# A hybrid decoder trunk: score masks as one product and one reduction, gates and row scale on ScalarE

## What is computed

```
def hgrn2(q, f_raw, i, g, lb, norm_w):
    f = lb + (1.0 - lb) * jax.nn.sigmoid(f_raw.astype(jnp.float32))
    log_f = jnp.log(f)
    k = 1.0 - f
    ...                       # scores_ij = sum_d q_id k_jd exp(cum_i - cum_j), j <= i
def mamba2(...):
    ...
    y = y.reshape(b, l, M_DIM) * jax.nn.silu(z.astype(jnp.float32))
    y = rms_norm(y.reshape(b, l, M_GROUPS, M_DIM // M_GROUPS)).reshape(b, l, M_DIM)
    return y * norm_w
```

## Time and profile before

| | |
|---|---|
| median of 3 runs | 2497.19 us (2496.18 to 2498.99) |
| the profiled execution's own time | 2498.01 us |
| its span, from the first to the last instruction | 2496.2 us |
| busy TensorE | 2392.7 us (96%) |
| busy VectorE | 1934.9 us (78%) |
| busy ScalarE | 1158.8 us (46%) |
| busy GpSimd | 167.4 us (7%) |

### The profile page before, as it was taken

How to read it: one execution, slowest core, us unless ns; L and a number is a source line. 1 busy time by engine, 2 the same in 40 slices (tenths; PEclk the granted TensorE clock), 3 DMA queues, 4 the chain that set the end, 5 groups by cost and what they waited for, 6 DMA issues and landing times.

```text
span 2496.2 us, 32892 instructions
## 1 busy us (share of the span) xinstructions
PE 2392.7 (96%) x13077; PEld 2071.0 (83%) x13077; DVE 1934.9 (78%) x2130; ACT 1158.8 (46%) x1504; POOL 167.4 (7%) x120
## 2 busy tenths in 40 slices
PE   2599999999999999999999999999999999999998
PEld 2599988888888888888879998888888888888886
DVE  7889898877898898889886578778888565655657
ACT  0264475545434435434436446655543443443442
POOL 0002100010011011010010110001001101101001
PEclk9999999999999999999999999999999999999999
DMA  9998577877898898999866546678788666656663
GB/s 388 393 336 300 148 267 261 292 273 270 291 345 308 290 348 306 316 315 313 296 201 177 155 118 202 225 261 282 253 289 301 188 190 193 186 189 192 186 192 119
DMA packets 205054, 633.78 MB, mean 254 GB/s; under 512 B 20237, under 2 KB 20965, under 8 KB 203621
## 3 DMA queue, kind: packets, MB, share of 16 engines
q1 hardware_dynamic: 200320, 614.80, 73.1%
q0 software_dynamic: 3008, 16.32, 1.7%
q10 hardware_dynamic: 1572, 0.56, 0.1%
HBM read 629.50 MB, written 2.10 MB: 253 GB/s over the span
## 4 chain that ended last, share of the span: by engine, by line
PE 90%; DVE 5%; DMA 2%; issue 1%; ACT 1%; SPq 0%; DVEq 0%; ACTq 0%
PE PS L1658 46%; PE PS L1684 17%; PE PS L1686 8%; PE PS L1626 8%; PE PS L1667 4%; DMA RAW<-in_w_ada 2%; PE PS L1640 2%; DVE ACC L1082 1%; DVE WL L1091 1%; PE PS L1715 1%; PE PS L1558 1%; PE PS L1591 1%; DVE CV L1298 0%; DVE ACC L985 0%; DVE MS L1315 0%
## 5 line engine op out<-in xcount | busy, mean ns | idle before, releaser
L686 ACT ACTIVATE WH<-RAW 128x1024 fp32r<-128x1024 f32 (+1 forms) x800 | 831.8, 1044 | 1082.6 <-PE PS L1658 554.6
L1091 DVE TENSOR_TENSOR WL<-RAW,WH 128x1024 fp32r<-128x1024 f32 (+1 forms) x800 | 992.0, 1247 | 431.8 <-ACT WH L686 430.6
L1684 PE MATMUL PS<-HT,WH 128*128 128x512 f32 x1792 | 632.5, 398 | 0.0
L1686 PE MATMUL PS<-HT,WL 128*128 128x256 f32 x1792 | 502.5, 280 | 0.0
L1684 PEld LDWEIGHTS PS<-HT,WH 128*128 128x128 f32 x1792 | 336.5, 188 | 82.3 <-issue 0.5
L985 DVE SCALAR_TENSOR_TENSOR ACC<-ADR,CT,ACC 128x1024 f32<-128x1024 f32 x300 | 392.0, 1307 | 12.3 <-DMA ADR<-in_w_ada 10.4
L1658 PE MATMUL PS<-WH,T2h 128*128 128x512 f32 x1208 | 374.2, 391 | 0.0
L1658 PE MATMUL PS<-WL,T2h 128*128 128x512 f32 x1208 | 372.1, 389 | 0.0
L1658 PE MATMUL PS<-WH,T2l 128*128 128x512 f32 x1208 | 372.0, 389 | 0.0
L1686 PEld LDWEIGHTS PS<-HT,WL 128*128 128x128 f32 x1792 | 338.4, 189 | 0.7 <-issue 0.5
L1658 PE MATMUL PS<-WH,HT 128*128 128x512 f32 x1024 | 288.7, 395 | 0.6 <-issue 0.6
(11 more groups left out here) (297 smaller groups left out, 2035.1 us busy)
## 6 DMA issues: line engine op xcount, KB each, us to landing
RAW<-in_w SPq DMA_DIRECT2D x512, 512.0 KB, 4.1
ADR<-in_w_ada SPq DMA_DIRECT2D x320, 512.0 KB, 5.5
RAW<-in_w_in SPq DMA_DIRECT2D x192, 512.0 KB, 3.9
RAW<-in_w_ada SPq DMA_DIRECT2D x64, 512.0 KB, 15.9
RAW<-in_w_out SPq DMA_DIRECT2D x64, 512.0 KB, 4.9
RAW<-in_w_in SPq DMA_DIRECT2D x32, 264.0 KB, 2.7
GB<-in_b_ada POOLq DMA_DIRECT2D x8, 512.0 KB, 7.3
LNG<-in_ln_g POOLq DMA_DIRECT2D x4, 1024.0 KB, 6.9
```

The lines of the kernel that those rows point to most:

```text
L686: act.activation(WH[:, wh_slot(layer, n), 0:w], RAW[:, k, 0:w], ACT.Copy).then_inc(hi_done.sem, 1)
L1091: tt(WL[:, k, 0:w], RAW[:, k, 0:w], WH[:, wh_slot(layer, n), 0:w].bitcast(F32), ALU.subtract).then_inc(lo_done.sem, 1)
L1684: mm(bank(p, j)[:, :], WH[:, wh, cols], HT[:, kt, :, :], start=kt == 0, stop=False, skip_group_check=True)
L1686: ins = mm(bank(p, j)[:, SEQ:2 * SEQ], WL[:, wl, cols], HTh[:, kt, :], start=False, stop=kt == KT - 1, skip_group_check=True)
```

## The change

The mask becomes one product over both PSUM banks (MS is written whole), and one `tensor_reduce` that adds the eight levels, reading MS with the level as the innermost index: neighbouring elements of the sum lie 128 floats apart. The gates go to ScalarE at (1,2), the logarithm moves from (1,4) to (1,3), the complement goes to ScalarE at (1,10). The scaling of XS goes to ScalarE at (7,4). The semaphores and their counts stay.

```
-                        if at == (1, 4):
+                        if at == (1, 2):
+                            act.wait_ge(set_free.sem, set_free.at(layer, 1))
+                            for h in range(4):
+                                fh = EQ[:, 2 * h:2 * h + 2, :]
+                                act.activation(fh, fh, ACT.Identity, bias=cLB[:, h:h + 1], scale=cOML[:, h:h + 1]
+                                               ).then_inc(hg_f.sem, 1)
+                        if at == (1, 3):
                             act.wait_ge(hg_f.sem, hg_f.at(layer, 4))
                             act.activation(E[:, :, :], EQ[:, :, :], ACT.Ln).then_inc(hg_lnf.sem, 1)
+                        if at == (1, 10):
+                            act.activation(KTt[:, :, :], EQ[:, :, :], ACT.Identity, bias=1.0, scale=-1.0
+                                           ).then_inc(hg_k.sem, 1)
...
+                        if at == (7, 4):
+                            act.wait_ge(rs_out.sem, rs_out.at(layer, 3))
+                            for b in range(4):
+                                xs = XS[:, b // 2, (b % 2) * 512:(b % 2 + 1) * 512]
+                                ins = act.activation(xs, xs, ACT.Copy, scale=RR[:, b:b + 1])
+                            ins.then_inc(m_rows.sem, 1)
...
                 dve.wait_ge(hg_s.sem, hg_s.at(layer, i + 1))
-                for b in range(2):
-                    ins = tt(MS[:, 4 * b:4 * b + 4, :], work(p, 2 + b)[:, :].rearrange("p (l i) -> p l i", i=P),
-                             LM[:, b * 512:(b + 1) * 512].rearrange("p (l i) -> p l i", i=P), ALU.mult)
-                ins.then_inc(hg_ms.sem, 1)
+                at = 4 * (1 - p % 2) + 2
+                tt(MS[:, :, :], PS[:, at:at + 2, :].rearrange("p b (l i) -> p (b l) i", i=P),
+                   LM[:, :].rearrange("p (l i) -> p l i", i=P), ALU.mult).then_inc(hg_ms.sem, 1)
                 dve.wait_ge(hg_ms.sem, hg_ms.at(layer, i + 1))
                 if i:
                     dve.wait_ge(hg_o.sem, hg_o.at(layer, i))
-                link(tt(MS[:, 0:4, :], MS[:, 0:4, :], MS[:, 4:8, :], ALU.add))
-                link(tt(MS[:, 0:2, :], MS[:, 0:2, :], MS[:, 2:4, :], ALU.add))
-                tt(SM[:, :], MS[:, 0, :], MS[:, 1, :], ALU.add).then_inc(hg_sm.sem, 1)
+                dve.tensor_reduce(SM[:, :], MS[:, :, :].rearrange("p l i -> p i l"), AX.X, ALU.add
+                                  ).then_inc(hg_sm.sem, 1)
...
-                        if at == (1, 3):
-                            dve.wait_ge(set_free.sem, set_free.at(layer, 1))
-                            for h in range(4):
-                                fh = EQ[:, 2 * h:2 * h + 2, :]
-                                ts(fh, fh, cOML[:, h:h + 1], cLB[:, h:h + 1], ALU.mult, ALU.add
-                                   ).then_inc(hg_f.sem, 1)
-                            dve.wait_ge(hg_f.sem, hg_f.at(layer, 4))
-                            ts(KTt[:, :, :], EQ[:, :, :], -1.0, 1.0, ALU.mult, ALU.add).then_inc(hg_k.sem, 1)
...
-                            dve.wait_ge(rs_out.sem, rs_out.at(layer, 3))
-                            for b in range(4):
-                                xs = XS[:, b // 2, (b % 2) * 512:(b % 2 + 1) * 512]
-                                ins = ts(xs, xs, RR[:, b:b + 1], None, ALU.mult)
-                            ins.then_inc(m_rows.sem, 1)
```

## The result

| | before | after |
|---|---|---|
| median of 5 runs each, us | 2497.19 | 2507.74 |
| lowest and highest run, us | 2495.17 to 2498.99 | 2506.25 to 2510.64 |
| profiled execution, us (its span) | 2498.01 (2496.2) | 2510.64 (2508.8) |

The changed kernel is slower: its time is 1.0042 times that of before, with an interval of 1.0031 to 1.0052, or +10.5 us. The prediction was 2496.9 us with a range up to 2502.5. It was wrong.

A forecast was written before the change was run, and what follows sets the result against it. TensorE, busy 2392.7 of 2496.2 us, was taken as the bound, so only its idle time could change. Mask -4.85, gates +3.55 and row scale +1.0 gave -0.3 us on the median 2497.19: 2496.9 us, range 2494.5 to 2502.5.

The forecast's parts named there:

- Part 1: Score mask: one product and one reduction of 1.22 us each end TensorE's waits for SM; -4.85 us.
- the stops at pass 4: First unit of pass 4, each layer: TensorE's 0.29 us stop for the product of mask 7 goes.
- rival (A): Score mask: the strided reduction is slow, 2.29 us at half rate; total +4.4, 2501.6 us; chance 0.19.
- Rival (B): Score mask: the reduction stops for GpSimd as the addition did; mask gives -1.5 us, total 2500.3 us; chance 0.07.
- Rival (D): Score mask: it gets shorter, but TensorE waits as long for something else; total 2501.7 us; chance 0.05.
- Part 2: Forget gates, logarithm and complement: ScalarE's late split makes TensorE wait ahead of unit (1,5) in layer 0; +3.55 us.
- the chain of three queues: Layer 0, (1,4): ScalarE's split holds VectorE's low-half split and the conditioning reduction behind it, then TensorE; reduction 3.55 us later.
- Rival (C): Unit (1,5): the 3.55 us do not appear, the conditioning result arriving some other way; total 2493.3 us; chance 0.09.
- Part 3: State-space row scale on ScalarE, both layers: later transposes and T2, only the larger delay counts; +1.0 us, between 0.4 and 1.6.
- The wait for XS: Ahead of TensorE's transposes, both layers: ScalarE's four scalings end at 492.2 instead of 491.3; 0.4 us of wait.
- The delay of T2l: Behind the split for (7,9): first low half of T2 ends at 499.5, TensorE takes it at 499.04; 0.5 us.

The follow-up runs named there:

- the mask alone: The kernel before with only the new score mask (one product, one strided reduction): 2496.66 us, ratio 1.0000.
- mask_woven: The kernel before with a new mask: TensorE writes four levels side by side into PSUM, so product and reduction read nearly in order: 2492.81 us, ratio 0.9980.
- gates_only: The kernel before with only the gates, logarithm and complement changed as in the changed kernel: 2504.43 us, ratio 1.0032.
- after_again: The changed kernel unaltered, run once more against the kernel before: 2502.42 us, ratio 1.0027.
- stall2: The kernel before with two dummy multiplications on VectorE ahead of the reduction of conditioning block 6 in layer 0: 2501.42 us, ratio 1.0022.
- stall3: The kernel before with three dummy multiplications on VectorE ahead of the reduction of conditioning block 6 in layer 0: 2503.4 us, ratio 1.0027.
- all_ln_late: The changed kernel with the logarithm moved back to (1,4), behind ScalarE's split for (1,8): 2496.85 us, ratio 1.0001 against the kernel before.
- woven_late: The kernel before with the mask of mask_woven, gates, complement and row scale on ScalarE, but the logarithm left at (1,4): 2494.53 us, ratio 0.9988.

## Why the prediction was wrong

**What bounds the kernel.** Right that only TensorE's idle time can be won. Wrong that only idle time can be lost: of the 12.6 us between the profiled executions 9.3 are busy time. The prediction doesn't read the clock of the kernel before, where it falls at the stops of the layer norms. TensorE's first products behind such a stop, and the window:

```profile
570.77 1.08 PE L1591 MATMUL PS<-K,X 128*128 128x128 f32 x4 [4.52 <-DVE X L1151]
```
```profile
570.00:575.00 5.00, 3.85 (x17) 3.51 (x18) 3.74 (x8) 2.88 (x5) 0.00 (x0) 0.50 1.01 395
```

So the trace had shown that a stop can be followed by half clock.

**Part 1, forecast -4.85 us, measured -0.4 by the times (the mask alone, within 2.5 us either way) and -2.0 by the starts.** The mis-sized term is the reduction: 2.01 us for 1.22. The working behind it was right, since the woven mask, which has the 1.22 us, gave -3.9 us by the times and -5.9 by the starts, took SM out of the list and left 0.2 us of the stops at pass 4. The choice of the row was the fault: the row of a reduction in order was taken for one with a step, though no row showed a step. Here rival (A) was right in its mechanism, a slow reduction; its 2.29 us for the reduction and its 0.15 us of gain were both too dark. The Trainium skill ("SBUF — State Buffer", "Specifications (TRN2)") says that an access needs a second hit in a line of 16 bytes. The traces agree: the steps of 512 and 32 bytes cost 0.79 and 0.90 us, and four neighbours together, in `mask_woven`, cost nothing; whether it is the line or the step as such, no run separates. Rival (B) is refuted: the reduction does not slow beside GpSimd (2.04 us at the most). Rival (D), that another wait takes the place of SM, is refuted by the woven mask too.

**Part 2, forecast +3.55 us, measured +7.4 alone.** The mechanism, its place, the chain of three queues and the size of the wait were right: it rose by 3.49 us, and the reduction started at 171.91 for the 171.55 worked out, in an execution that was 0.4 us late by then. The step that failed is the one after it, that the wait costs only its length. What follows the wait was put at nothing: half clock for 3.4 or 6.8 us, in which the products cost another 1.3 to 1.6 us (gates_only, after_again, `stall2`) or 2.8 us (after, `stall3`). Moving that one conditioning step ahead of the split takes the loss away to within the scatter; moving the logarithm back leaves a wait that cost 1.1 us. Rival (C), no wait, is refuted. What is left of the 7.4 us, and of the +10.5 us of the first series, lies in part in the falls of pass 5 (1.6 us in the profile of gates_only, 4.8 us in that of after).

**Part 3, forecast +1.0 us, measured +0.8.** The wait for XS is 0.35 to 0.37 us in each layer by the list and 0.54 us by the starts, where 0.4 was worked out; the four scalings take 2.55 us, 0.64 each, where 0.62 was. The delay of T2l, which was to be the larger of the two with 0.5 us, shows neither in the list nor in the starts (0.03 us at the most). So the sum of 1.0 us is right by the starts (1.1 us), but by the other of its two terms.

**The sum.** By the terms as measured alone it is -0.4 + 7.4 + 0.8 = +7.8 us. The two series of the changed kernel lie on either side, at +10.5 and +5.7. The clock falls in pass 5, 4.8 us in the first profile and none in the second, are as large as this gap, and the longer half clock at (1,5) adds 1.3 us. Whether these alone made it wasn't settled: the clock is known window by window for the profiled executions only. The waits alone, by the starts, make -2.0 + 3.5 + 1.1 = +2.6 us where the prediction had -0.3; the half clock at (1,5) adds 1.3 to 2.8 us.

## What to carry over

A wait of a few microseconds on a TensorE that was running without a gap has to be priced above its length, because of the slow products behind it: 1.4 to 1.8 times in the five profiles here, 1.7 to 2.1 times by the medians. The wait that grew by 1.1 us cost its length. When a step is moved to an engine, look for what another engine has queued behind it: here one conditioning step behind a late split made most of the loss, and changing its place in the queue mended it. And a layout with a step is not priced by a row in order: let the engine that pays nothing for the step, here TensorE writing to PSUM, make the order that the others read.

## What the runs showed of the hardware

- The granted clock fell from 2.4 to 1.2 GHz at each 2.5 to 3.7 us wait of TensorE that a profile here shows at (1,5) (five profiles of four kernels), for 3.4 or 6.8 us by the windows (a PEclk of 0.66 in one window of 5 us, or 0.75 and 0.56 in two). The same wait of 3.4 us had 6.8 us of it in after and 3.4 us in after_again. Behind 1.05 us it did not fall (all_ln_late, woven_late). Behind waits of 0.9 to 2 us, the two of pass 5 and the one of 2.0 us for SM in layer 1, it fell in some executions and not in others.
- VectorE in float32 over 1024 elements: 1.22 us in order, 2.01 us where a reduction reads SBUF 512 bytes apart, 2.12 us where a product writes SBUF 32 bytes apart, 1.22 us where a reduction reads runs of four neighbours. Neither step cost a factor of two.
- TensorE's output into PSUM 16 bytes apart took 275 ns per product of 128 columns, one every 112 ns, as without a step. The Trainium skill ("PSUM — Partial Sum Buffer", "Specifications (TRN2)") says that a pattern that isn't contiguous slows matmuls significantly; for these float32 products the trace does not show it.
- The reduction, with one SBUF input, kept its time beside GpSimd's multiplication, where the addition with two inputs had been stretched from 0.69 to 1.53 us.
